# A mixture of experts on one core: the last expert's rows added on TensorE through a transposed one-hot, the other experts' rows gathered beside it, and the last norm shared by ScalarE and VectorE

## What is computed

```python
probs = softmax(xt @ w_router + b_router)              # 16 experts in 4 groups
# one group per token, the top 2 experts in it, weights renormed to 1 -> gates (tokens, 16)
for e in range(16):
    he = silu(xt @ w_gate[e]) * (xt @ w_up[e])
    y = y + gates[:, e:e + 1] * (he @ w_down[e])
x = layernorm(alpha * x + y, ln2_g, ln2_b)             # alpha = 2 ** 0.25
```

## Time and profile before

| | |
|---|---|
| median of 3 runs | 1223.18 us (1222.6 to 1224.28) |
| the profiled execution | 1224.94 us |
| its span, first to last instruction | 1222.8 us |
| TensorE busy | 1125.5 us, 92% |
| VectorE busy | 948.7 us, 78% |
| ScalarE busy | 637.8 us, 52% |
| one copy `mhi` (ScalarE), mean of 192 | 1.915 us |
| one remainder `mlo` (VectorE), mean of 192 | 2.289 us |
| one remainder `lo` of the first half, mean of 56 | 2.290 us |
| HBM traffic in the expert loop | 374 to 384 GB/s |
| TensorE's granted clock, mean | 0.967 of 2.4 GHz |

### The profile page before, as it was taken

One profiled execution on the slowest core, in us unless ns is written; L12 is line 12 of the kernel. 1 busy time (PEld: TensorE's weight loads), 2 busy tenths in 40 slices (PEclk: granted clock), 3 DMA queues, 4 the chain that ended last, 5 costly groups with the idle time before them and its releaser, 6 DMA issues.

```text
span 1222.8 us, 15178 instructions
## 1 busy us (share of the span) xinstructions
PE 1125.5 (92%) x5857; PEld 877.5 (72%) x5857; DVE 948.7 (78%) x1011; ACT 637.8 (52%) x582; POOL 127.5 (10%) x223
## 2 busy tenths in 40 slices
PE   2999999999999999997789999999999999999950
PEld 2986986897798689985667676767766676767630
DVE  3498798889889883555668888888888888888836
ACT  3342343234143224531267777777777777777730
POOL 3020220220112030000120000000000000000011
PEclk9999999999999999999589999999999999999985
DMA  8672974685397394454299999999999999999923
GB/s 176 192 250 91 300 263 155 205 276 205 140 284 240 105 286 161 133 180 164 82 352 366 375 374 381 379 382 381 380 380 380 380 384 381 380 379 381 373 83 97
DMA packets 171259, 331.84 MB, mean 271 GB/s; under 512 B 8459, under 2 KB 45627, under 8 KB 171169
## 3 DMA queue, kind: packets, MB, share of 16 engines
q1 hardware_dynamic: 150704, 264.41, 61.6%
q0 software_dynamic: 20480, 66.42, 16.7%
HBM read 294.88 MB, written 36.63 MB: 271 GB/s over the span
## 4 chain that ended last, share of the span: by engine, by line
PE 79%; DVE 11%; DMA 4%; ACT 3%; issue 2%; POOL 1%; SPq 0%; POOLq 0%; DVEq 0%; ACTq 0%
PE bank L726 74%; PE bank L767 3%; DVE lo L1081 3%; DVE cT L1382 2%; DMA x_in<-in_x_prompt_dram 1%; ACT hi L1076 1%; PE bank L970 1%; DMA x_slots<-x,slot 1%; DVE st L1518 1%; POOL x_slots L684 1%; DMA y_back<-y_slots,slot 1%; DMA xg_tok<-x_slots 1%; DMA y_slots<-yo 1%; DVE o_tok L1480 0%; DVE stats L1472 0%
## 5 line engine op out<-in xcount | busy, mean ns | idle before, releaser
L1668 DVE TENSOR_TENSOR mlo<-mraw,mhi 128x2048 fp32r<-128x2048 f32 x192 | 439.3, 2289 | 79.5 <-ACT mhi L1254 76.1
L1254 ACT ACTIVATE mhi<-mraw 128x2048 fp32r<-128x2048 f32 x192 | 367.5, 1915 | 91.7 <-PE bank L726 85.1
L726 PE MATMUL bank<-mhi,xg_hi 128*96 128x512 f32 x512 | 203.1, 397 | 1.4 <-DVE xg_lo L1673 1.4
L726 PE MATMUL bank<-mhi,xg_lo 128*96 128x512 f32 x512 | 202.8, 396 | 0.0
L726 PE MATMUL bank<-mlo,xg_hi 128*96 128x512 f32 x512 | 201.6, 394 | 0.0
L1076 ACT ACTIVATE hi<-raw 128x2048 fp32r<-128x2048 f32 x47 | 89.9, 1913 | 196.5 <-PE bank L726 174.2
L1081 DVE TENSOR_TENSOR lo<-raw,hi 128x2048 fp32r<-128x2048 f32 x56 | 128.1, 2290 | 80.1 <-ACT hi L1076 45.5
L726 PE MATMUL bank<-xT_hi,hi 128*128 128x336 f32 x512 | 165.4, 323 | 6.4 <-DVE lo L1081 6.4
L726 PE MATMUL bank<-xT_hi,lo 128*128 128x336 f32 x512 | 163.5, 319 | 0.0
L726 PE MATMUL bank<-xT_lo,hi 128*128 128x336 f32 x512 | 163.2, 319 | 0.0
L1382 DVE SCALAR_TENSOR_TENSOR cT<-W,vec,cT 128x336 f32<-128x336 f32 x240 | 118.5, 560 | 0.0
(11 more groups left out here) (252 smaller groups left out, 1501.6 us busy)
## 6 DMA issues: line engine op xcount, KB each, us to landing
mraw<-in_w_gate_dram SPq DMA_DIRECT2D x64, 1024.0 KB, 10.6
mraw<-in_w_up_dram SPq DMA_DIRECT2D x64, 1024.0 KB, 10.5
mraw<-in_w_down_dram SPq DMA_DIRECT2D x64, 1024.0 KB, 11.6
raw<-in_w_in_dram SPq DMA_DIRECT2D x40, 1024.0 KB, 6.5
st<-in_state_ret_dram POOLq DMA_DIRECT2D x32, 512.0 KB, 4.9
out_dram<-st POOLq DMA_DIRECT2D x32, 512.0 KB, 4.5
raw<-in_w_ret_o_dram SPq DMA_DIRECT2D x8, 1024.0 KB, 5.8
x_slots<-zeros POOLq DMA_DIRECT2D x12, 512.0 KB, 4.3
```

The source lines that it names most:

```text
L726: i = pe.matmul(out, a, b, start=s, stop=e)
L1254: act.activation(mhi[:, v % MH, :], mraw[:, v % MR, :], ACT.Copy).then_inc(mhi_ready, 1)
L1668: dve.tensor_tensor(mlo[:, v % MH, :], mraw[:, v % MR, :], mhi[:, v % MH, :].bitcast(f32), ALU.subtract).then_inc(mlo_ready, 1)
```

## The change

The last expert's rows no longer pass through HBM. From `rank` and the gates VectorE makes, early in the first pair, a weighted one-hot for the last expert (`apart`, into `picks`, free by then), and for the other fifteen the slots and weights with those of the last set to zero (`early_slot`, `early_w`). At the last pair's start TensorE transposes the one-hot, and ScalarE copies it to `back` (96 x 336). GpSimd waits for the store of expert 14 only and gathers the two rows per token of the fifteen while expert 15 is computed; tile 0 goes where `xg_tok` was, tiles 1 and 2 into the weight slots 0 and 1, once these have been used for the last time. VectorE adds them to `y` behind its last remainder. TensorE puts `y` of tile 0 into two PSUM banks by an identity product (`carried`), ahead of the last unit; behind it come `back` x `yo` on top, and both for tiles 1 and 2. The norm reads PSUM: statistics on VectorE, the normalising on ScalarE (Identity with scale and bias per row), gamma on VectorE in halves. The loads of gamma and beta move ahead of the loop.

```diff
-        LAST = Stage(PAIR, expert_groups(0, 1) + expert_groups(1, 0))
+        LAST = Stage(PAIR, ["Pback"] + expert_groups(0, 1) + expert_groups(1, 0))
+
+        FIN = Stage(LAST, ["Ff00", "Ff01", "Pf10", "Pf11", "Ff20", "Ff21"])
...
+            sp.dma_start(ln2_bc[:, 0, :], ln2_g.to_broadcast([TT, D])).then_inc(s_ln2, 16)
+            sp.dma_start(ln2_bc[:, 1, :], ln2_b.to_broadcast([TT, D])).then_inc(s_ln2, 16)
             sp.wait_ge(most_ready, 1)
...
-            sp.wait_ge(moe_done, 1)
-            sp.dma_start(ln2_bc[:, 0, :], ln2_g.to_broadcast([TT, D])).then_inc(s_ln2, 16)
-            sp.dma_start(ln2_bc[:, 1, :], ln2_b.to_broadcast([TT, D])).then_inc(s_ln2, 16)
...
-                for p in range(2):
-                    stored(LAST, p, 0)
-                    pool.dma_start(y_slots[(NE - 2 + p) * CAP:(NE - 1 + p) * CAP, :], yo[:, p, :]).then_inc(yo_stored, 16)
-                pool.wait_ge(yo_stored, 16 * NE)
+                stored(LAST, 0, 0)
+                pool.dma_start(y_slots[(NE - 2) * CAP:(NE - 1) * CAP, :], yo[:, 0, :]).then_inc(yo_stored, 16)
+                pool.wait_ge(yo_stored, 16 * (NE - 1))
+                pool.wait_ge(early_ready, 1)
+                pool.wait_ge(group_done, LAST.done("xt01"))
 
                 for t in range(NT):
+                    if t:
+                        pool.wait_ge(mlo_ready, U_PAIR.idx(15 + t, NE // 2 - 1) + 1 + MLEAD)
                     for k in range(2):
-                        pool.indirect_dma_start(y_back[:, 2 * t + k, :], None, y_slots, bass.IndirectOffsetOnAxis(slot[:, k, t:t + 1], 0)
+                        o = y_back12[:, 2 * (t - 1) + k, :] if t else y_back0[:, k, :]
+                        pool.indirect_dma_start(o, None, y_slots[0:(NE - 1) * CAP, :], bass.IndirectOffsetOnAxis(early_slot[:, k, t:t + 1], 0)
                                                 ).then_inc(gathered[t], 16)
...
+                def carried(t):
+
+                    for n in range(2):
+                        pe.matmul(bank[FIN.bank[f"f{t}{n}"]][0:TT, :], ident[0:TT, 0:TT], y[:, t, 512 * n:512 * n + 512], start=True, stop=False)
...
+                            if stage is LAST and p and kh and n:
+                                for q in range(2):
+                                    room(FIN, f"f0{q}", 0)
+                                pe.wait_ge(summed, 1)
+                                carried(0)
                             half(stage, v + 8 + 2 * kh + n, it, wit, f"d{p}{n}", kh, hT_hi, hT_lo)
...
                 pe.wait_ge(turned, NE // 2)
+                pe.wait_ge(back_ready, NT)
+                turn(LAST, "back", 0, [(bank[LAST.bank["back"]][0:CAP, t * TT:(t + 1) * TT], picks[:, t, :], TT) for t in range(NT)])
                 expert(LAST, 0, 0, NE // 2 - 1, True)
                 expert(LAST, 1, 0, NE // 2 - 1, False)
+                evacuated(LAST, "back", 0)
+                for t in range(NT):
+                    if t:
+                        for n in range(2):
+                            room(FIN, f"f{t}{n}", 0)
+                        pe.wait_ge(summed, t + 1)
+                        carried(t)
+                    for n in range(2):
+                        evacuated(LAST, f"d1{n}", 0)
+                        pe.matmul(bank[FIN.bank[f"f{t}{n}"]][0:TT, :], back[:, t * TT:(t + 1) * TT], yo[:, 1, 512 * n:512 * n + 512],
+                                  start=False, stop=True).then_inc(group_done, 1)
...
+                b, e = full(LAST, "back")
+                act.activation(back[:, :], b[0:CAP, 0:T], ACT.Copy).then_inc(e, 1)
                 expert(LAST, 0, 0, NE // 2 - 1, True)
                 expert(LAST, 1, 0, NE // 2 - 1, False)
+                for t in range(NT):
+                    act.wait_ge(rv_ready, NORMS + 2 + NT + t)
+                    act.activation(mmv[:, t, 3:4], mmv[:, t, 2:3], ACT.Sqrt).then_inc(rstd_done, 1)
+                    act.wait_ge(shift_ready, t + 1)
+                    for n in range(2):
+                        b = bank[FIN.bank[f"f{t}{n}"]]
+                        act.activation(y[:, t, 512 * n:512 * n + 512], b[0:TT, :], ACT.Identity, scale=mmv[:, t, 3:4], bias=mmv[:, t, 1:2]).then_inc(y_scaled, 1)
...
+                def apart():
+
+                    for k in range(2):
+                        f = gs[:, 1 + k, :]
+                        link(dve.tensor_tensor(last_w[:, k, :], gt[:, 3 * k + 3, :, NE - 1], gs[:, 3 + 2 * k, :], ALU.mult))
+                        link(dve.scalar_tensor_tensor(early_w[:, k, :], f, float((NE - 1) * CAP), gs[:, 3 + 2 * k, :], ALU.is_lt, ALU.mult))
+                        link(dve.scalar_tensor_tensor(f, f, float((NE - 1) * CAP), f, ALU.is_lt, ALU.mult))
+                    dve.tensor_copy(early_slot[:, :, :], gs[:, 1:3, :]).then_inc(early_ready, 1)
+                    link(dve.tensor_tensor(last_w[:, 0, :], last_w[:, 0, :], last_w[:, 1, :], ALU.add))
+                    for t in range(NT):
+                        dve.tensor_scalar(picks[:, t, :], row[:, :], rank[:, 1, t:t + 1], last_w[:, 0, t:t + 1], ALU.is_equal, ALU.mult).then_inc(back_ready, 1)
...
+                        if stage is PAIR and it == 0 and p == 0 and u == 6:
+                            apart()
...
-                for n in range(2):
-                    dve.wait_ge(*took(LAST, f"d1{n}"))
-                dve.sem_inc(moe_done, 1)
-
                 for t in range(NT):
                     dve.wait_ge(gathered[t], 32)
                     for k in range(2):
-                        g = gs[:, 3 + 2 * k, t:t + 1]
-                        link(dve.scalar_tensor_tensor(y[:, t, :], y_back[:, 2 * t + k, :], g, y[:, t, :], ALU.mult, ALU.add))
+                        src_ = y_back12[:, 2 * (t - 1) + k, :] if t else y_back0[:, k, :]
+                        i = dve.scalar_tensor_tensor(y[:, t, :], src_, early_w[:, k, t:t + 1], y[:, t, :], ALU.mult, ALU.add)
...
+                dve.wait_ge(s_ln2, 32)
+                for t in range(NT):
+                    for n in range(2):
+                        b, e = full(FIN, f"f{t}{n}")
+                        link(dve.bn_stats(mst[:, t, 6 * n:6 * n + 6], b[0:TT, :]))
+                    link(dve.bn_aggr(mmv[:, t, 0:2], mst[:, t, 0:12]))
+                    link(dve.tensor_scalar(mmv[:, t, 2:3], mmv[:, t, 1:2], EPS, None, ALU.add))
+                    dve.reciprocal(mmv[:, t, 2:3], mmv[:, t, 2:3]).then_inc(rv_ready, 1)
+                    dve.wait_ge(rstd_done, NORMS + 1 + NT + t + 1)
+                    dve.scalar_tensor_tensor(mmv[:, t, 1:2], mmv[:, t, 0:1], -1.0, mmv[:, t, 3:4], ALU.mult, ALU.mult).then_inc(shift_ready, 1)
+                    for n in range(2):
+                        c = slice(512 * n, 512 * n + 512)
+                        dve.wait_ge(y_scaled, 2 * t + n + 1)
+                        i = dve.tensor_tensor(y[:, t, c], y[:, t, c], ln2_bc[:, 0, c], ALU.mult)
+                        if t < NT - 1:
+                            if n:
+                                i.then_inc(normed, 1)
+                        else:
+                            link(i)
+                            i = dve.tensor_tensor(y[:, t, c], y[:, t, c], ln2_bc[:, 1, c], ALU.add)
+                            if n:
+                                i.then_inc(normed, 1)
```

More of the change, by code:

```diff
@@ L283, in program @@
         picks = sb("picks", [TT, NT, CAP])
-        rank = sb("rank", [TT, NT])
+        rank = sb("rank", [TT, 2, NT])
+        last_w = sb("last_w", [TT, 2, NT])
+        early_slot = sb("early_slot", [TT, 2, NT], mybir.dt.int32)
+        early_w = sb("early_w", [TT, 2, NT])
+        back = sb("back", [CAP, T])
         most_i = sb("most_i", [TT, 1], mybir.dt.int32)
@@ L308, in program @@
         base[0] = phase + 2 * 4 * NT * D
-        y_back = sb("y_back", [TT, 2 * NT, D])
+        y_back12 = sb("y_back12", [TT, 4, D])
+        base[0] = phase + 2 * 4 * NT * D + MR * 8192
+        y_back0 = sb("y_back0", [TT, 2, D])
         base[0] = phase
@@ L406, in program @@
         gathered = [sem(f"gathered{t}") for t in range(NT)]
-        picks_ready = sem("picks_ready")
+        picks_ready, back_ready, early_ready, summed = (sem(n) for n in ("picks_ready", "back_ready", "early_ready", "summed"))
+        shift_ready, y_scaled = sem("shift_ready"), sem("y_scaled")
         xg_full = [sem(f"xg_full{i}") for i in range(2)]
@@ L411, in program @@
         chosen_ready = sem("chosen_ready")
[L412 removed]
+        yo_stored, yo_free = sem("yo_stored"), sem("yo_free")
         y_ready, moved_up = sem("y_ready"), sem("moved_up")
@@ L1316, in _ @@
                             act.activation(h_hi[:, 2 * j:2 * j + 2, :], h_f[:, :, :], ACT.Copy).then_inc(hhi_ready, 1)
-            for t in range(NT):
-                act.wait_ge(rv_ready, NORMS + 2 + NT + t)
-                act.activation(mmv[:, t, 3:4], mmv[:, t, 2:3], ACT.Sqrt).then_inc(rstd_done, 1)
+                for t in range(NT):
+                    act.wait_ge(rv_ready, NORMS + 2 + NT + t)
```

(27 more changed lines are left out.)

5 lines of the change are left out of this document (2 added, 3 removed).

## The result

| | before | after |
|---|---|---|
| median of the runs, us | 1223.73 (1222.6 to 1226.81) | 1213.76 (1212.65 to 1216.41) |
| profiled execution, its span, us | 1224.94, 1222.8 | 1216.41, 1214.5 |
| end of the last norm on VectorE | 1217.09 | 1209.39 |

A forecast was written before the change was run, and what follows sets the result against it. TensorE, busy 92% of the span, was taken as the bound, with a 38.87 us tail behind it. Sums' end 1182.7 + norm 15.5 = 1198.2 instead of 1217.09, 18.9 us earlier: median 1204.3 us, range 1202 to 1209.

The forecast's parts named there:

- the 0.35 allowed for the transposes: Last pair's start: three 112x96 transposes on TensorE cost 0.35 us (bounds 0.2 and 0.5), all on the path.
- 2.75 MB at 380 GB/s are 7.2 us; even if they went ahead of every weight, unit 23 would land by about 1169.4: Last expert: gathers beside the weight stream delay its last weight unit, wanted at 1170.3, by 0, at most 1 us.
- hidden behind the sums, with 1 us to spare: Before the last unit: TensorE loses 2.9 us waiting for tile 0's sums, covered by VectorE's six sums.
- a 512-column f32 product at 0.43 us: Identity products on TensorE: 0.43 us each, 0.86 us a pair, 1.7 us for tiles 1 and 2 each.
- the clock rival: TensorE, idle from 1175.8 to 1177.5, falls to 1.2 GHz; second statistic 2.5 us late, 1207 us; chance 0.06.
- The sums took 7.63 us against 7.86: VectorE behind the last remainder: six sums of 1.31 us, 7.86 us in all, ending at 1182.7.
- the rival of late gathers: Last expert: each gather needs its whole 0.93 us free, so the last tile's sums end at 1189.3; 1211 us, chance 0.09.
- The norm took 15.64 against 15.5: Final norm of three tiles: 14.27 + 1.2 = 15.5 us, bounds 14.3 and 16.5.
- No table load stands between root and Identity: Rival in the norm: ScalarE changes tables in each tile, 3.3 us exposed; 1208 us, chance 0.05.
- the new addresses: Rival in the expert loop: shifted buffers lengthen VectorE's remainders, at 2.80 us each giving 1240 us; chance 0.03.
- Back-to-back remainders do not let it through: Last expert: an indirect DMA begun inside a VectorE remainder waits for its end, and passes only at an opening between operations.
- the forecast's pace: Last expert: one gather for each VectorE opening, the first near 1151.6, the sixth ending near 1169.6 and landing by 1177.3.

The follow-up runs named there:

- e9: The changed kernel with its six gathers replaced by three 1 MB weight-tile loads issued by GpSimd, which the sums read: 1208.1 us.
- e7: The changed kernel with tile 0's gathers early, the other four after the last weight tile's landing, and tile 0's identity products behind the last unit: 1204.83 us.
- e2: The changed kernel without its six gathers; VectorE adds y itself in place of each gathered row: 1205.34 us.
- e3: The changed kernel with GpSimd waiting for the last weight tile's landing before its first gather: 1206.91 us.
- e10: The changed kernel with only tiles 1 and 2's four gathers waiting for the last weights' landing, TensorE's order unchanged: 1207.37 us.
- e1: The changed kernel with the gamma and beta loads issued in the middle of the expert loop instead of ahead of it: 1215.5 us.

## Why the prediction was wrong, step by step

In profiled executions E was forecast at 1198.2 and came at 1209.39: 11.2 us. By the marks: S 4.84 later, S to L 3.91 longer than 29.16 (3.55 of it beyond the 0.35 allowed for the transposes), L to N 2.64 longer than 7.86, N to E 0.14. One of the prediction's own signs of being wrong came: the last weights' copies on ScalarE waited for their transfer.

**The step that failed first** is "2.75 MB at 380 GB/s are 7.2 us; even if they went ahead of every weight, unit 23 would land by about 1169.4", with its value of 0. It is a sum of the right kind with two wrong terms. The first is the rate: 380 is the weights' own. At the 251 GB/s of before's gathers, a row that stood in the trace of before and that I did not use, 2.75 MB are 11 us. The second is the place that it starts from: the traffic had thinned out by 1162, but unit 23 landed only at 1163.7. With both set right it lands near 1174.7, against the 1170.3 at which ScalarE wanted it: 4.4 us late where 3.9 were measured. The same working fits the others: e9's 3.15 MB at 384 GB/s are 8.2 us, 1.6 us late (1.5 measured), and e7's two gathers at 251 are 3.7 us and in time (as measured). With the right place alone the rate of 380 would have made 0.7 us. e2, e3 and e7 show the loss away once less, or nothing, goes beside the stream, and e9 that the rate is the rows', not the queue's.

**The second** is TensorE's cover, "hidden behind the sums, with 1 us to spare". The term under it, a 512-column f32 product at 0.43 us, was half of what it is: the row's x6 are records, two to a product. Unit 23 then ends 0.86 us later. (Tiles 1 and 2 want 3.4 us of TensorE each and not 1.7, still less than a tile's norm, 4.7.) And both products with `back` stand behind it in TensorE's order (1192.62 in after), so that the first statistic, too, waits for unit 23 and another 0.86 us; I had let only the second one depend on it. e2 and e10 measured 0.80 and 0.81 us of waiting. The other 2.1 us are the clock rival's, which I had held off with the earlier trace rows for 1.7 us of idle time. With the weights in time it did not come (e2, e3 and e10, idle for 1.78, 1.78 and 1.82 us). It came as a consequence of the first step, and its price (2.5 us at the second statistic) was near. My list of cases gave it 0.06, as if by itself, and the late weights, which bring it, had no case at all.

**The first pair.** S was 4.84 us later in this one execution. The first scatter began at 606.76 (606.52 before), but the rows were in `x_slots` and `xg_tok` could be asked for only at 629.72 (628.15 before):

```profile
629.72 0.57 POOL L695 DMA_DIRECT2D xg_tok<-x_slots  x1 [9.91 <-DMA x_slots<-x,slot]
...
637.97 1.51 PE L778 MATMUL bank<-tab,xg_tok 96*128 96x96 f32 x8 [2.88 <-DMA xg_tok<-x_slots]
```

TensorE's transposes waited for it, 2.88 us where the earlier trace rows had 1.68, and began 2.08 us later. In that wait the granted clock fell, as it had not before; the same two windows, first of the change, then of before:

```profile
638.00:642.00 4.00, 4.00 (x15) 3.11 (x16) 3.86 (x5) 0.98 (x2) 0.00 (x0) 0.50 1.05 388
642.00:646.00 4.00, 4.00 (x15) 2.70 (x14) 0.00 (x0) 1.44 (x1) 0.00 (x0) 0.73 1.05 388
```

```profile
638.00:642.00 4.00, 4.00 (x19) 2.82 (x18) 2.53 (x5) 1.92 (x1) 0.00 (x0) 1.00 1.05 386
642.00:646.00 4.00, 4.00 (x22) 2.86 (x21) 4.00 (x3) 2.48 (x3) 0.00 (x0) 1.00 1.05 354
```

The transposes and unit 6 took 6.33 us and not 3.47. So the 4.84 us are about 2 of a later transfer and 2.9 of the clock. The issue lies ahead of `apart()`'s operations (633.81 to 636.06), the only ones the change adds there. Over the twelve traces S goes with that issue: at 626.7 and 626.8 it is 1143.6 and 1144.3, at 627.7 to 628.9 1144.7 to 1147.3, from 629.4 on 1148.7 to 1150.2. From the second copy of the first expert's `yo` to S there are 491.4 to 491.6 us in all twelve, so the transposes and `back` of the last pair, priced at 0.35 us, cost nothing that shows.

The medians should hold less of this, yet they hold some. Take the time from S to the end of each profiled execution (79.60 us before, 66.23 after) from the kernel's median, as if that time were the same in every execution. This puts S at 1144.1 to 1144.6 before, at 1147.5 after, and at 1144.9 to 1147.2 in e1 to e10. The forecast for the median had it at 1143.6. So of the 9.5 us by which the median missed, 6.4 lie between S and E, 3.9 ahead of S, and behind E 0.8 were won that I had not forecast. All eleven changed kernels come out later ahead of S than before, by 1.6 us in the mean, so the change may cost something there. But all these differences rest on the one trace of before, and no run settles it; e1, whose S comes out at 1146.5, gives no sign that it is the gamma and beta loads.

**What held.** The sums took 7.63 us against 7.86, without a wait, and with them the rival of late gathers falls. The norm took 15.64 against 15.5. No table load stands between root and Identity: the only one behind the experts is at 1193.43, 1.28 us, ahead of its wait; Identity took 0.77 us a half, against 0.75. By the Trainium skill's rule (ScalarE: Activation LUTs, "Table sets: the hidden batching unit"), that identity is in every set, the trace agrees. Remainders took 2290 ns, so the new addresses cost nothing.

**Right for a partly wrong reason.** "Back-to-back remainders do not let it through" is refuted. The second gather, begun at 1157.69 inside the first of two back-to-back remainders (1157.02 + 4.65 for both), ended at 1160.12, 0.8 us behind their boundary near 1159.3. The gathers were thus faster than the openings allowed. By the forecast's pace the last of them would have run behind the weights, so the right result, gathers in time, came by a way that put more traffic beside the stream. What held the first scatter for 5.11 us, in every trace, is open.

## What to carry to other kernels

Price a transfer put beside a full stream by the rate that this very kind of transfer shows, at its share of the DMA engines, and not by the stream's rate, and start from the landing of the last load. What this stream lost it had not got back four pairs later (e1), so moved traffic belongs behind the last load, and only what is needed first goes ahead. Count products, not records, when a merged row is divided. A cover of 1 us that rests on another step being in time is no case of its own: when that step failed here, the cover failed with it, and the clock fell too.

## What the runs showed of the hardware

Gathers of 448 KB in 4 KB rows from `y_slots` run at about 250 GB/s of full engine time, by proportion (186 at a share of 0.74 in before; 165 at 0.68 in 1168 to 1172 of e3), a stream of 1 MB weight tiles at 387 (share 1.05, 1130 to 1150 of before). Plain rows were seen only mixed with weights, at 319. While both are under way, GpSimd's transfers delay weights that were queued before them: unit 22's load, issued at 1153.84 and so 2.6 us before the first gather, landed after 19.7 us and not 11.7.

An indirect DMA issued by GpSimd beside VectorE's remainders ended about 0.8 us behind the remainder that was running when it began, again at a boundary between two back-to-back ones, and no remainder was lengthened. The Trainium skill (SBUF — State Buffer, "SBUF: two separate sides") has whichever of the two starts first hold the shared ports for its whole instruction. The trace agrees where the remainder came first. Where the gather was under way it does not: the remainder of 1164.96 began 0.29 us before the gather of 1162.76 had ended, and took its usual 2.29 us.

A 512-column f32 product on TensorE is two records and 0.86 us at 2.4 GHz (1194.41 to 1196.13 for two, in the changed kernel).
